# A transformer block kernel whose late transposes are split over the two halves of TensorE's array

## The reference

```python
# layers 0 and 1 (FFN_DIM = 2816)
h = rms_norm(x, ffn_norm_w[layer])
gu = h @ w_gate_up[layer]
x = x + (jax.nn.silu(gu[..., :FFN_DIM]) * gu[..., FFN_DIM:]) @ w_down[layer]
...
# the third layer (inner width 4096)
h = rmsnorm(x, norm_mlp_g[i])
x = x + jnp.square(jax.nn.relu(h @ mlp_w1[i].astype(dt))) @ mlp_w2[i].astype(dt)
return rmsnorm(x, norm_final_g)
```

## Time and profile before

| | |
|---|---|
| median of 3 runs | 1283.19 us (1282.0 to 1283.58) |
| profiled execution, its own time | 1282.6 us |
| its span in the trace | 1281.3 us |
| TensorE busy | 1267.6 us, 7010 matmuls |
| VectorE busy | 815.8 us |
| ScalarE busy | 692.3 us |
| granted TensorE clock | 9 tenths or more in all 40 slices |
| `ffn_turn`, line 571 | 22 calls, 88 transposes |
| `mlp_turn`, line 973 | 16 calls, 64 transposes |

### The profile page before, as it was taken

The page is one execution under the profiler, slowest core; times in us unless marked ns, Lnnn a source line. Parts: engine busy times, 40 slices in busy tenths (PEclk is TensorE's granted clock), DMA queues, the critical chain, the costliest instruction groups (busy, mean ns, idle before and its releaser), DMA issues.

```text
span 1281.3 us, 17290 instructions
## 1 busy us (share of the span) xinstructions
PE 1267.6 (99%) x7010; PEld 1050.2 (82%) x7010; DVE 815.8 (64%) x1094; ACT 692.3 (54%) x1023; POOL 114.8 (9%) x109
## 2 busy tenths in 40 slices
PE   8999999999999999999999999999999999999998
PEld 6888888888877888888888888888888888888886
DVE  5657755556787566555567989746876764654453
ACT  6665544443877545444457665445854454644443
POOL 1110000000220010000000213010320000100001
PEclk9999999999999999999999999999999999999999
DMA  8755466764545556666644543333547544556561
GB/s 286 222 162 173 152 216 200 256 197 164 163 163 168 185 156 222 197 197 197 193 142 157 158 141 98 101 101 97 150 149 263 165 152 131 182 189 199 171 201 56
DMA packets 119216, 220.17 MB, mean 172 GB/s; under 512 B 8304, under 2 KB 54128, under 8 KB 119136
## 3 DMA queue, kind: packets, MB, share of 16 engines
q1 hardware_dynamic: 115312, 206.08, 50.6%
q0 software_dynamic: 2672, 10.20, 2.5%
q10 hardware_dynamic: 1152, 2.78, 0.6%
HBM read 215.88 MB, written 3.15 MB: 171 GB/s over the span
## 4 chain that ended last, share of the span: by engine, by line
PE 96%; DMA 1%; ACT 1%; DVE 1%; issue 0%; SPq 0%; ACTq 0%; DVEq 0%
PE ps L349 27%; PE ps L351 27%; PE ps L350 27%; PE ps L712 3%; PE ps L366 2%; PE ps L571 1%; PE ps L701 1%; PE ps L690 1%; PE ps L961 1%; PE ps L973 1%; PE ps L519 1%; PE ps L946 1%; DMA raw<-in_w_gate_up 0%; PE ps L673 0%; PE ps L662 0%; PE ps L378 0%
## 5 line engine op out<-in xcount | busy, mean ns | idle before, releaser
L1446 DVE TENSOR_TENSOR spl<-raw,spl 128x1024 fp32r<-128x1024 f32 x387 | 471.6, 1241 | 158.1 <-ACT spl L994 156.9
L994 ACT CAST spl<-raw 128x1024 fp32r<-128x1024 f32 x387 | 400.4, 1050 | 188.1 <-PE ps L351 89.4
L349 PE MATMUL ps<-spl,xs 128*128 128x512 f32 x1056 | 422.0, 400 | 0.0
L351 PE MATMUL ps<-spl,xs 128*128 128x512 f32 x1056 | 412.1, 390 | 0.0
L350 PE MATMUL ps<-spl,xs 128*128 128x512 f32 x1056 | 411.2, 389 | 0.0
L351 PEld LDWEIGHTS ps<-spl,xs 128*128 128x128 f32 x1056 | 198.2, 188 | 42.5
L349 PEld LDWEIGHTS ps<-spl,xs 128*128 128x128 f32 x1056 | 198.4, 188 | 40.7 <-issue 1.8
L350 PEld LDWEIGHTS ps<-spl,xs 128*128 128x128 f32 x1056 | 198.7, 188 | 39.0 <-issue 0.5
L349 PE MATMUL ps<-spl,ys 128*128 128x512 f32 x496 | 200.9, 405 | 0.1
L351 PE MATMUL ps<-spl,ys 128*128 128x512 f32 x496 | 194.5, 392 | 0.0
L350 PE MATMUL ps<-spl,ys 128*128 128x512 f32 x496 | 193.8, 391 | 0.0
(11 more groups left out here) (306 smaller groups left out, 1048.4 us busy)
## 6 DMA issues: line engine op xcount, KB each, us to landing
raw<-in_w_in SPq DMA_DIRECT2D x112, 512.0 KB, 3.9
raw<-in_w_gate_up SPq DMA_DIRECT2D x176, 256.0 KB, 4.2
raw<-in_mlp_w SPq DMA_DIRECT2D x64, 512.0 KB, 4.3
raw<-in_w_down SPq DMA_DIRECT2D x44, 512.0 KB, 4.4
raw<-in_w_out SPq DMA_DIRECT2D x24, 512.0 KB, 3.7
raw<-in_xattn_wk SPq DMA_DIRECT2D x8, 512.0 KB, 4.0
raw<-in_xattn_wv SPq DMA_DIRECT2D x8, 512.0 KB, 3.7
raw<-in_w_branch_gdn SPq DMA_DIRECT2D x8, 512.0 KB, 3.8
```

What stands on the lines that cost most here:

```text
L349: self.do.matmul(bank, xh, hi, start=start, stop=False)
L351: m = self.do.matmul(bank, xl, hi, start=False, stop=stop)
L994: self.do.copy(self.k.spl[:, u % NH, 0, :], self.k.raw[:, u % NR, :]).then_inc(*self.up("hi", (u,)))
L1446: self.do.tensor_tensor(lo, self.k.raw[:, u % NR, :], hi.bitcast(F32), ALU.subtract).then_inc(*self.up("lo", (u,)))
```

## The change

The two functions that turn the feed-forward's product and the MLP's inner layer no longer transpose 128x128 at once. Each transpose becomes two, one of partitions 0 to 63 (64 tokens) and one of partitions 64 to 127, with the corner of the identity that belongs to them. The first writes to one bank, the second to another; the calls alternate between them. Each of the two banks then holds 256 columns in place of one bank's 512, is cast by ScalarE and subtracted by VectorE by itself, and is freed by itself. The values and where they end up in `ys` are as before. The semaphore counts go up once per bank on ScalarE and VectorE, and once per call on TensorE as before.

```diff
+    def ffn_places(self, l, b, g):
+
+        o = self.k.x["ys"][:, :, 2 * (b % 4):2 * (b % 4) + 2, :].rearrange("p l k (t n) -> p l k t n", t=2)
+        return o[:, :, :, :, HALF[g]], self.ps("ft", l, b, g)[:, 0:256].rearrange("p (k t n) -> p k t n", k=2, t=2)
+
+    def mlp_places(self, b, t, g):
+        o = self.k.x["ys"][:, :, 4 * (b % 2):4 * (b % 2) + 4, t * P + 64 * g:t * P + 64 * g + 64]
+        return o, self.ps("mt", b, t, g)[:, 0:256].rearrange("p (k n) -> p k n", k=4)
...
     # Tensor
     def ffn_turn(self, l, b):
         s = self.s2(f"act{b}")
-        bk = self.hold("ft", l, b)
+        bk = [self.hold("ft", l, b, g) for g in range(2)]
         for t in range(2):
             self.wait_ge(*self.at("dm", ("gu", l, b), t))
             for f in range(2):
-                m = self.do.transpose(bk[:, f * 256 + t * P:f * 256 + (t + 1) * P], s[:, t, f * P:(f + 1) * P],
-                                      self.ident())
+                for g, r in enumerate(HALF):
+                    m = self.do.transpose(bk[g][:, f * P + t * 64:f * P + (t + 1) * 64], s[r, t, f * P:(f + 1) * P],
+                                          self.ident()[r, r])
         m.then_inc(*self.up("mx", ("ft", l, b)))
-        self.let(("ft", l, b), "xl", "ft", l, b)
+        for g in range(2):
+            self.let(("ft", l, b, g), "xl", "ft", l, b, g)
...
     def mlp_turn(self, b, t):
         s = self.s2(f"m{b}")
-        bk = self.hold("mt", b, t)
+        bk = [self.hold("mt", b, t, g) for g in range(2)]
         self.wait_ge(*self.at("pm", ("up", b), t))
         for f in range(4):
-            m = self.do.transpose(bk[:, f * P:(f + 1) * P], s[:, t, f * P:(f + 1) * P], self.ident())
+            for g, r in enumerate(HALF):
+                m = self.do.transpose(bk[g][:, f * 64:(f + 1) * 64], s[r, t, f * P:(f + 1) * P], self.ident()[r, r])
         m.then_inc(*self.up("mx", ("mt", b, t)))
-        self.let(("mt", b, t), "xl", "mt", b, t)
+        for g in range(2):
+            self.let(("mt", b, t, g), "xl", "mt", b, t, g)
...
     # Scalar, ffn_turn (mlp_turn alike)
-        o = self.k.x["ys"][:, 0, 2 * (b % 4):2 * (b % 4) + 2, :]
-        self.do.copy(o, self.psg(2, "ft", l, b)).then_inc(*self.up("xh", ("ft", l, b)))
+        for g in range(2):
+            o, v = self.ffn_places(l, b, g)
+            self.do.copy(o[:, 0], v).then_inc(*self.up("xh", ("ft", l, b, g)))
...
     # Vector, ffn_turn (mlp_turn alike)
-        v = self.k.x["ys"][:, :, 2 * (b % 4):2 * (b % 4) + 2, :]
-        self.wait_ge(*self.at("xh", "ft", l, b))
-        self.do.tensor_tensor(v[:, 1], self.psg(2, "ft", l, b), v[:, 0].bitcast(F32),
-                              ALU.subtract).then_inc(*self.up("xl", ("ft", l, b)))
+        for g in range(2):
+            o, v = self.ffn_places(l, b, g)
+            self.wait_ge(*self.at("xh", "ft", l, b, g))
+            self.do.tensor_tensor(o[:, 1], v, o[:, 0].bitcast(F32),
+                                  ALU.subtract).then_inc(*self.up("xl", ("ft", l, b, g), ("ft", l, b)))
```

More of the change, by code:

```diff
@@ L1416, in mlp_turn @@
             self.wait_ge(*self.at("mm", ("dn", b - 2), 1))
-        o = self.k.x["ys"][:, 0, 4 * (b % 2):4 * (b % 2) + 4, t * P:(t + 1) * P]
-        self.do.copy(o, self.psg(4, "mt", b, t)).then_inc(*self.up("xh", ("mt", b, t)))
+        for g in range(2):
+            o, v = self.mlp_places(b, t, g)
+            self.do.copy(o[:, 0], v).then_inc(*self.up("xh", ("mt", b, t, g)))
     def finish_squares(self, t, j):
@@ L1905, in mlp_turn @@
     def mlp_turn(self, b, t):
[L1906 to L1909, removed]
+        for g in range(2):
+            o, v = self.mlp_places(b, t, g)
+            self.wait_ge(*self.at("xh", "mt", b, t, g))
+            self.do.tensor_tensor(o[:, 1], v, o[:, 0].bitcast(F32),
+                                  ALU.subtract).then_inc(*self.up("xl", ("mt", b, t, g), ("mt", b, t)))
     def finish_x(self, t, j, *done):
```

## The result

The changed kernel takes 1287.89 us (median of 6 runs, 1287.29 to 1288.35) against 1282.97 us for the kernel before (6 runs, 1280.96 to 1283.81). The ratio is 1.004, with a 95% interval of 1.0027 to 1.0053: slower by 4.9 us, where 4.7 were forecast.

What follows compares the result with a forecast made beforehand. TensorE's stream was taken to bound the kernel. 36 turns at +0.14 us and two layer ends at -0.15 sum to +4.7 us, added to 1283.19 for 1287.9 us; range 1286.0 to 1297.0.

Steps and rivals of the forecast that it cites:

- Where the time is: Whole span: TensorE is busy for 99%, so a microsecond on its stream is one of the result, barring nearby waits.
- The step: Turns on TensorE: alternating half-height transposes step at 0.029 us, so 8 stream in 0.23 us against 0.445 for 4 old ones.
- In and out: Around each turn on TensorE: going from full-height to half-height work and back costs 0.355 us.
- The turn: Each plain turn on TensorE: 0.587 us against 0.445, 0.14 us more, bounds 0.12 to 0.19.
- The layer ends: Last turn of each of two feed-forward layers: the 0.30 us stall on VectorE goes, 0.15 us less each.
- Evacuation and banks: ScalarE casts and VectorE subtracts, 7 and 5 us extra in all, and bank reuse with 4.4 us of room: costed at nothing.
- Rival (c): Extra ScalarE and VectorE instructions eat the lead of the weight splits, so TensorE waits: +12 us, 1295; chance 5%.
- Rival (a): The halves don't overlap for transposes, so a turn costs 0.82 us: +14 us, 1297; chance 9%.
- Rival (b): The mode change isn't paid, so a turn costs 0.23 us: gain 8.1 us, 1275; chance 6%.
- (d): Transposes overlap but something else in the turn moves it to about the threshold: no change; chance 5%.

Runs made afterwards that it cites:

- one_half_only: The changed kernel, but all 8 transposes of a turn read partitions 0 to 63, leaving the lower half idle; 1299.79 us.
- two_banks_full: The kernel before with two banks a turn and halved casts and subtracts, but full-height transposes; 1282.46 us, ratio 0.9994.
- wide_groups_half: The kernel before with half height for the convolution's 48 way-back transposes and the 64 of the delta rule's operands; 1281.9 us, ratio 0.9991.
- half_by_half: The changed kernel, but each turn runs all upper-half transposes first, then all lower-half ones, without alternating; 1291.69 us, ratio 1.0063.
- half_by_half_x4: The changed kernel with every transpose issued four times, 16 on the upper half and then 16 on the lower; 1348.9 us.

## Why the prediction was right

**Where the time is.** The total and the distances moved together, 4.9 us and 38 distances. That TensorE's stream is the result was right to within the 0.45 us at the start that no part of the change explains. The agreement to 0.01 us is luck: the forecast added 4.7 us to 1283.19, where six runs of the kernel before give 1282.97, and the trace's sum of +4.8 us has 35 turns slightly above the forecast and one 0.34 us below it.

**The step.** 0.029 us forecast, 0.031 measured. Taking it from alternating 64x64 work was right, and that it means two halves side by side, each at 0.058, is borne out by one_half_only at 0.061.

**In and out.** 0.355 and 0.365 us from the earlier trace rows, 0.345 measured. This term decided the sign: the saving in the stream is 0.436 - 8 x 0.031 = 0.19 us (0.213 forecast), and the price is larger. That transposes don't escape it, which the earlier trace rows showed by L641 alone, held for every turn. One reading in the prediction doesn't hold: that the 0.355 us are "the same stall" as the weight load's pause of 0.35 us. The pause runs for the most part while the product ahead is still at work, and delays the first transpose by 0.09 us only; the other 0.25 us of the price come behind the first transpose, before the second product. The two figures are near each other, but one doesn't measure the other. The forecast took its price from start times, so it didn't suffer.

**The turn.** +0.14 us forecast, +0.15 measured, inside 0.12 to 0.19.

**The layer ends.** Forecast -0.15 each, measured -0.12 and -0.13, with the stall gone, as foreseen. two_banks_full takes as much (0.15) from these two places at full height, by its own layout of the banks. With half height TensorE arrives later and the stall has gone but for 0.03 us, so the two reasons don't add.

**Evacuation and banks.** Costed at nothing; two_banks_full is 0.9994 of before. Rival (c) is out in these turns. That banks cost nothing held here because there was room; in wide_groups_half, where a split group takes more banks than before, TensorE waited for them.

**Rival (a)**, no overlap, would have shown 1.27 us a turn and shows up as one_half_only at 1.29. **Rival (b)**, no price for the change of height, would have shown 0.69. **(d)** would have needed a cheaper turn; none of 37 is off by more than 0.01 us.

**What the sum had wrong:** the turn early in layer 1, which it counted as a plain turn at +0.14 us. It waits for the gating, and that for a weight's DMA; its distance was 1.76 us before, 1.56 after, and 0.9 to 3.7 us in the experiments with four tiles a turn, full height or half. It is the largest single scatter between executions that I found, and here it moved the result by 0.2 us.

## What to carry to other kernels

Working on half of the array's rows has a fixed price each time that the engine goes there from full-height work and back, here 0.345 us, and a gain by the piece, here 0.047 us a transposed 128x128 tile; below about seven tiles in a row it loses, so count the tiles between two changes before splitting. A group that is at half height already isn't free to join either, if the shape of its tiles differs. And two halves write to two banks: where a group takes more banks than before, see who still reads the next ones. In a stream that the engine sets, read the price of small matmuls from the distance between the neighbours on both sides, at two group lengths; the recorded durations (235 ns for a half, 272 for a whole) show neither the fixed price nor the steps of 0.031 and 0.109 us.

## What the runs showed of the hardware that was not expected

TensorE took transposes of the other half from three or four places further on in the program, and ran them beside the first half's; sixteen places further on it did not. So alternation needn't be exact, but it must be near.

A wait of TensorE may cost more than itself. In half_by_half the turn in layer 1 waited for both gatings and a late DMA together, 2.1 us as recorded, and after it the granted clock was at the lower level (1.2 GHz), 0.67 as a mean over 489 to 494 us:

```profile
488.94 0.70 PE L582 MATMUL ps<-con,ar 64*128 64x64 f32 x8 [2.13 <-DVE ar L1640]
...
490.59 0.63 PE L360 MATMUL ps<-spl,xs 128*128 128x512 f32 x1
491.01 0.63 PE L358 MATMUL ps<-spl,xs 128*128 128x512 f32 x1
```

Products are 0.42 to 0.43 us apart here, and 0.23 again from 492.30 on. half_by_half_x4 has it behind the same turn, which waited 1.56 us (0.69 over 506 to 511 us). That the wait is the cause isn't shown: 1.46 us in wide_groups_half left the clock at the higher level. In the same execution of half_by_half the clock was low once more, 0.66 over 880 to 885 us, without any wait, behind a group of 64x64 matmuls and one on 16 rows; no other of the twelve traces has that, so it isn't explained. Against the changed kernel's trace the wait makes 2.2 us, the two slow stretches some 1.0 and 1.6, the turns 0.4; the spans differ by 4.6 us (1291.2 and 1286.6), with a start that was 0.4 us earlier.
